# A cache page loaded into 32 partitions in pieces of 8 KB instead of 128 partitions in pieces of 2 KB

## The chip, the cores and the metric

The kernel runs on one core of one Trainium2 chip (trn2). The metric is the device time of one execution in microseconds (us). Three runs were timed before the change; the profile is of one further execution. TensorE is called PE, its weight load PEld, VectorE DVE, ScalarE ACT, GpSimd POOL and SyncE SP.

## What is computed

The reference is one inference step of a hybrid decoder layer: modulation of the input by a conditioning vector, one input projection, a short gated convolution beside differential attention with four heads, one output projection, two normalisations and a dense channel mixer. It does this for a prompt of 1,024 tokens and for eight sequences of four new tokens each. The eight sequences attend to 8,192 past keys each, which lie in pages of 128 keys; a table says which pages belong to a sequence. The part that matters here, cut:

```python
k_past = cache_k[l, page_table].reshape(bs, past, N_HEADS, 2, QK_HEAD)
v_past = cache_v[l, page_table].reshape(bs, past, N_HEADS, V_HEAD)
...
s = jnp.einsum('bqhcd,bkhcd->bhcqk', q, k).astype(jnp.float32) * (QK_HEAD ** -0.5)
p = jax.nn.softmax(s, axis=-1)
a = p[:, :, 0] - lam * p[:, :, 1]
return jnp.einsum('bhqk,bkhd->bqhd', a, v.astype(jnp.float32))
```

A page of keys is 128 rows of 512 float32 numbers (four heads of 128), 256 KB in one piece of memory; a page of values is the same. Eight sequences have 64 pages of either kind, so 1,024 pages or 268.4 MB are read.

## The kernel before

The kernel works in stages one after another: the modulation vectors; the input projection; the attention; the output projection; the channel mixer's first half; its second half. Only the attention stage reads the cache. There the prompt's attention and that of the eight sequences are woven into each other, written out by hand.

The attention stage is a row of eight steps. Step b scores the 64 key pages of sequence b and, beside that, weighs the 64 value pages of sequence b - 1 whose softmax is finished; step 0 has keys only, and after the last softmax there is a stretch with values only. Within a step the pages are taken in 16 groups of four, four rounds r of four groups g, and into each round one tile of the prompt's attention is woven. At the start of a step stands the softmax of the sequence before, a chain through DVE, PE and ACT.

Two rings hold the pages, `k_ring` (L230) and `v_ring` (L231), each of 128 partitions and four slots; a slot holds one group of four pages, 1 MB. The loads are issued by `load_pages` (L440). SP issues the groups with g = 0 and 2, POOL those with g = 1 and 3, each in the order keys of group g, values of group g, next g. Before every page the issuing engine reads its number from `page_row` (L445, a load from memory into a register); before the first page of a group it waits until the slot is free (L448); then it issues one load per page (L449). The four loads of a group raise the slot's semaphore by 16 each.

- `turn_keys` (L1428, its instruction L1432) waits until the four key pages of a slot are there, and turns them on DVE in blocks of 32 x 32 into `k_turned`; that frees the key slot.
- `key_group` (L845, its matmuls L852) multiplies the turned keys by the queries on PE, 32 matmuls for a group; ACT then copies the scores to `s_rows` (L1103).
- `value_group` (L857, its matmuls L862) waits until the four value pages of a slot are there and weighs them on PE by the turned scores `p_t`; that frees the value slot.

In the ring before, page j of a group lies in columns j of the slot, and key i of the page in partition i. Keys, scores, weights and values use that same place throughout, so which key of the group has which place doesn't matter as long as keys and values agree.

Two other loads are named below. `ada_bias` (L490) in the first stage is a vector of 6,144 numbers copied into 32 partitions, 24 KB each. `xs_rows` (L506) loads the 32 sample rows of 1,024 numbers into 32 partitions, 4 KB each; SP issues it after the prompt's rows `x_rows` (L504) and before the first weights `w_raw` (L500), which both go to all partitions.

Of the kernel before, what the change touches and what calls it, by code (L numbers as in the profile page):

```python
# [34 lines left out]
ds = bass.ds  # L35

P = 128
QUAD = 32
BANK = 512
# [72 lines left out]
def build(nc, z, io, const_at, n_const):  # L112
    T, D, B, S, H, HD, F = z.T, z.D, z.B, z.S, z.H, z.HD, z.F
# [5 lines left out]
    GP, RING = 4, 4  # L119
    REVS = z.PAGES // (GP * RING)  # L120
    NEW0 = z.PAGES * QUAD
    SC = NEW0 + QUAD
    assert z.MODS * D // BANK == 2 * z.MODS
    NG = F // WB
    NB_IN, NB_OUT = z.IN // WB, D // WB
    lam_init = 0.8 - 0.6 * math.exp(-0.3 * 0)
# [1 line left out]
    with ExitStack() as ctx:  # L128
# [311 lines left out]
        def load_pages(eng, par):  # L440


            def group(pages, ring, landed, free, b, r, g):
                for j in range(GP):
                    page = eng.value_load(page_row[0:1, ds((b * REVS + r) * (RING * GP) + (g * GP + j), 1)],  # L445
                                          min_val=0, max_val=z.POOL - 1)
                    if j == 0:
                        eng.wait_ge(free, (b * REVS + r) * RING + g + 1)  # L448
                    eng.dma_start(ring[:, g, j, :], pages[ds(page, 1)].rearrange("o p d -> p (o d)")  # L449
                                  ).then_inc(landed[g], 16)  # L450

            keys, values = (k_pages, k_ring, k_in, k_free), (v_pages, v_ring, v_in, v_free)
            with eng.Fori(0, REVS) as r:
                for g in range(par, RING, 2):
                    group(*keys, 0, r, g)
            with eng.Fori(0, B - 1) as b:
                with eng.Fori(0, REVS) as r:
                    for g in range(par, RING, 2):
                        group(*keys, b + 1, r, g)
                        group(*values, b, r, g)  # L460
            with eng.Fori(0, REVS) as r:
                for g in range(par, RING, 2):
                    group(*values, B - 1, r, g)
# [1237 lines left out]
```

## Time and profile before

| | us |
|---|---|
| median of 3 runs | 2386.14 (2381.53 to 2386.65) |
| span of the profiled execution, first to last instruction | 2380.2 |
| attention stage in it, from the first page ordered to the last value matmul | 428 to 1300 |
| PE busy | 1984.2 (83%) |
| DVE busy | 1056.3 (44%) |
| POOL busy | 354.0 (15%) |

The profile follows one execution. Times in its rows are from the start of the span. The columns of the views are told where each first stands. A row on transfers counts what all 16 DMA engines moved; their busy share is a mean over the 16 and counts a packet from its start to its end in the slice in which it starts, so that short slices can show more than 1. The time to landing of a load runs from its issue until its semaphore has its full count.

### The profile page before, as it was taken

To read this page: it belongs to the slowest core of one execution; us is meant where nothing else is said; L and a number is where in the kernel's file an instruction comes from. 1 tells how busy PE (TensorE), PEld (TensorE's weight loads), DVE (VectorE), ACT (ScalarE), POOL (GpSimd) and SP (SyncE) were. 2 spreads that over 40 slices of the span, in tenths; PEclk is the share of its full clock that TensorE was granted. 3 is DMA by queue.
4 is the path that set the end of the run, shared out by engine and by line. 5 is a ranking of instruction groups with operands and counts; after the bars stand their busy time and mean duration, and the time that the engine had idled before them with its cause. 6 is when DMAs were issued, how large, how long until landed. Compare 5 with 4: busy or idle time off the path is not lost.

```text
span 2380.2 us, 47877 instructions
## 1 busy us (share of the span) xinstructions
PE 1984.2 (83%) x17492; PEld 1635.0 (69%) x17492; DVE 1056.3 (44%) x1528; ACT 486.3 (20%) x831; POOL 354.0 (15%) x544
## 2 busy tenths in 40 slices
PE   4699999668786876878785794999999997999992
PEld 1277898557665765767674793777777776888881
DVE  2424211666675665766561557111111112455457
ACT  0300111021212112121221203111211111333331
POOL 0000000223242423324232104200000000000003
PEclk7799999799897988889796896999999998999996
DMA  9711223779897979879896410121212123411112
GB/s 302 256 36 35 72 71 118 250 245 341 285 385 282 385 279 346 314 283 381 298 354 234 156 35 18 54 71 53 88 53 70 53 88 128 137 41 37 36 32 91
DMA packets 210968, 404.21 MB, mean 170 GB/s; under 512 B 24426, under 2 KB 88938, under 8 KB 210788
## 3 DMA queue, kind: packets, MB, share of 16 engines
q1 hardware_dynamic: 161012, 261.51, 31.9%
q0 software_dynamic: 41488, 136.35, 15.5%
q10 hardware_dynamic: 8320, 4.19, 0.6%
q8 instruction: 116, 1.90, 0.3%
q14 instruction: 32, 0.26, 0.0%
HBM read 377.53 MB, written 24.51 MB: 169 GB/s over the span
## 4 chain that ended last, share of the span: by engine, by line
PE 65%; DVE 13%; SPq 7%; DMA 7%; issue 6%; ACT 1%; DVEq 0%; ACTq 0%
PE psum L753 26%; PE psum L1002 11%; PE psum L761 10%; PE psum L852 5%; DVE k_turned L1432 4%; SPq L445 4%; SPq L449 3%; DMA ada_w<-w_ada 3%; DMA k_ring<-cache_k 3%; PE psum L1009 2%; PE psum L862 2%; DVE p_t L424 2%; PE psum L736 2%; PE psum L832 1%; DVE x_lo L1282 1%
## 5 line engine op out<-in xcount | busy, mean ns | idle before, releaser
L852 PE MATMUL psum<-k_turned,q_blocks 128*32 128x128 f32 x4096 | 332.3, 286 | 85.6 <-DVE k_turned L1432 84.9
L852 PEld LDWEIGHTS psum<-k_turned,q_blocks 128*32 128x32 f32 x4096 | 291.7, 114 | 137.1 <-issue 98.5
L1432 DVE STREAM_TRANSPOSE k_turned<-k_ring 128x2048 f32<-128x2048 f32 x128 | 295.4, 2308 | 6.6 <-DMA k_ring<-cache_k 5.7
L753 PE MATMUL psum<-x_hi,w_hi 128*128 128x512 f32 x896 | 281.3, 395 | 0.0
L753 PE MATMUL psum<-x_lo,w_hi 128*128 128x512 f32 x896 | 277.3, 391 | 0.0
L753 PE MATMUL psum<-x_hi,w_lo 128*128 128x512 f32 x896 | 276.0, 389 | 0.0
L1301 DVE TENSOR_TENSOR w_lo<-w_raw,w_hi 128x2048 fp32r<-128x2048 f32 x37 | 86.9, 2350 | 363.1 <-ACT w_hi L1057 353.5
L1002 PE MATMUL psum<-d_hi,h_hi 128*128 128x256 f32 x704 | 209.2, 297 | 12.2 <-DVE d_lo L1646 11.1
L862 PE MATMUL psum<-v_ring,p_t 128*32 128x128 f32 x4096 | 191.7, 295 | 19.3 <-DMA v_ring<-cache_v 18.9
L1002 PE MATMUL psum<-d_lo,h_hi 128*128 128x256 f32 x704 | 199.9, 284 | 0.0
L1002 PE MATMUL psum<-d_hi,h_lo 128*128 128x256 f32 x704 | 199.7, 284 | 0.0
L753 PEld LDWEIGHTS psum<-x_hi,w_hi 128*128 128x128 f32 x896 | 165.6, 188 | 44.8 <-ACT h_out L1193 4.5
L449 POOL DMA_DIRECT2D k_ring<-cache_k x256 | 138.5, 541 | 371.5 <-issue 189.0
L753 PEld LDWEIGHTS psum<-x_lo,w_hi 128*128 128x128 f32 x896 | 168.8, 188 | 35.7
L753 PEld LDWEIGHTS psum<-x_hi,w_lo 128*128 128x128 f32 x896 | 168.5, 188 | 35.9
L761 PE MATMUL psum<-w_hi,x_hi 128*128 128x256 f32 x640 | 182.4, 285 | 0.0
L761 PE MATMUL psum<-w_hi,x_lo 128*128 128x256 f32 x640 | 181.3, 283 | 0.0
L761 PE MATMUL psum<-w_lo,x_hi 128*128 128x256 f32 x640 | 181.2, 283 | 0.0
L1645 DVE TENSOR_TENSOR h_lo<-h_all,h_hi 128x1024 fp32r<-128x1024 f32 x88 | 107.6, 1223 | 145.8 <-ACT d_hi L1218 145.8
L449 POOL DMA_DIRECT2D v_ring<-cache_v x256 | 138.4, 541 | 217.6 <-issue 170.0
L1002 PEld LDWEIGHTS psum<-d_hi,h_hi 128*128 128x128 f32 x704 | 135.1, 192 | 48.2 <-issue 45.0
L862 PEld LDWEIGHTS psum<-v_ring,p_t 128*32 128x32 f32 x4096 | 147.7, 117 | 27.9 <-DMA v_ring<-cache_v 25.8
(228 smaller groups left out, 2525.1 us busy)
## 6 DMA issues: line engine op xcount, KB each, us to landing
k_ring<-cache_k SPq DMA_DIRECT2D x256, 256.0 KB, 8.0
k_ring<-cache_k POOLq DMA_DIRECT2D x256, 256.0 KB, 6.1
v_ring<-cache_v SPq DMA_DIRECT2D x256, 256.0 KB, 8.8
v_ring<-cache_v POOLq DMA_DIRECT2D x256, 256.0 KB, 6.0
ada_w<-w_ada SPq DMA_DIRECT2D x12, 2048.0 KB, 9.6
w_raw<-w_in SPq DMA_DIRECT2D x12, 1024.0 KB, 5.3
w_raw<-w_gate SPq DMA_DIRECT2D x11, 1024.0 KB, 5.4
w_raw<-w_up SPq DMA_DIRECT2D x11, 1024.0 KB, 6.3
```

The costliest lines, as they stand in the source:

```text
L424: last = copy(to[QUAD * a:QUAD * (a + 1), :, j], got[:, :, :, a, :])
L445: page = eng.value_load(page_row[0:1, ds((b * REVS + r) * (RING * GP) + (g * GP + j), 1)], min_val=0, max_val=z.POOL - 1)
L449: eng.dma_start(ring[:, g, j, :], pages[ds(page, 1)].rearrange("o p d -> p (o d)")).then_inc(landed[g], 16)
L736: last = mm(psum[q:q + QUAD, 4 + s, 0:WB], x_t_s[:, k, :], w_raw[:, s, k, :], start=k < 4, stop=k >= KC - 4)
L753: last = mm(psum[:, 2 * ft + c, 0:CH], w[:, s, k, ft * P:(ft + 1) * P], x[:, k, c * CH:(c + 1) * CH], start=k == 0 and j == 0, stop=k == K ...
L761: last = mm(psum[:, t % TB, 0:WB], x[:, k, t * P:(t + 1) * P], w[:, s, k, :], start=k == 0 and j == 0, stop=k == KC - 1 and j == 2)
L852: last = mm(psum[QUAD * h:QUAD * (h + 1), g % 2, 0:GP * QUAD], q_blocks[:, h, d, :], k_turned[:, g % 2, :, h * HD + d * QUAD:h * HD + (d + ...
L862: last = mm(psum[QUAD * h:QUAD * (h + 1), 2, 0:P], p_t[:, (r * RING + g) * GP + j, :], v_ring[:, g, j, h * HD:(h + 1) * HD], start=False, ...
L1002: last = mm(psum[:, down_bank(par, pair), (t % 2) * WB:(t % 2 + 1) * WB], x[:, s, t * P:(t + 1) * P], w[:, s, :], start=k == 0 and j == 0 ...
L1301: v.tensor_tensor(w_lo[:, s], w_raw[:, s], w_hi[:, s], ALU.subtract).then_inc(w_lo_done, 1)
L1432: v.transpose(k_turned[:, g % 2].rearrange("p j n -> p (j n)"), k_ring[:, g].rearrange("p j n -> p (j n)")).then_inc(k_free, 1)
L1645: v.tensor_tensor(h_lo[:, s, :], h_all[:, k, :], h_hi[:, s, :], ALU.subtract)
```

## The change

A load of a page writes 32 partitions in place of 128. Page j of a group goes to partitions 32 j to 32 j + 31, and each of these partitions takes four consecutive key rows, 8 KB, which fill its whole slot. So a group of four pages still fills the same slot of 1 MB, and the four pages stand below one another rather than beside one another. A load has 32 pieces of 8 KB where it had 128 of 2 KB. No instruction of PE, DVE or ACT is added, removed, moved or changed in shape; SP and POOL issue as many loads as before in the same order with the same waits.

```diff
-    assert z.MODS * D // BANK == 2 * z.MODS
+    assert z.MODS * D // BANK == 2 * z.MODS and z.PAGE == QUAD * GP
...
-                    eng.dma_start(ring[:, g, j, :], pages[ds(page, 1)].rearrange("o p d -> p (o d)")
-                                  ).then_inc(landed[g], 16)
+                    eng.dma_start(ring[QUAD * j:QUAD * (j + 1), g].rearrange("p i d -> p (i d)"),
+                                  pages[ds(page, 1)].rearrange("o (p i) d -> (o p) (i d)", i=GP)).then_inc(landed[g], 16)
```

The constants are QUAD = 32 and GP = 4, the pages of a group.

## Rows read from the trace of the kernel before

**Rows 1.** The page: span, and data rate in 40 equal slices of it.

```profile
span 2380.2 us, 47877 instructions
...
GB/s 302 256 36 35 72 71 118 250 245 341 285 385 282 385 279 346 314 283 381 298 354 234 156 35 18 54 71 53 88 53 70 53 88 128 137 41 37 36 32 91
```

**Rows 2.** Stretches: us, busy time by engine, PE's clock, DMA share, GB/s.

```profile
428.00:523.00 95.00, 62.57 (x641) 50.57 (x642) 65.66 (x91) 15.01 (x43) 26.82 (x49) 0.90 0.84 280
523.00:619.00 96.00, 76.80 (x1157) 64.51 (x1155) 63.35 (x90) 18.16 (x48) 32.31 (x61) 0.92 0.91 327
...
931.00:1043.00 112.00, 83.38 (x1192) 70.12 (x1192) 66.69 (x102) 21.07 (x57) 35.63 (x66) 0.88 0.90 327
...
428.00:1300.00 872.00, 652.66 (x9338) 545.12 (x9342) 533.95 (x770) 165.29 (x439) 278.01 (x513) 0.88 0.88 316
```

**Rows 3.** Stretches within a step: streaming, then the softmax, then the start again.

```profile
570.00:630.00 60.00, 47.70 (x669) 40.42 (x665) 37.41 (x48) 14.77 (x37) 22.59 (x42) 0.97 1.03 383
630.00:640.00 10.00, 2.74 (x42) 1.96 (x42) 7.96 (x21) 1.12 (x2) 0.00 (x0) 0.55 0.02 9
640.00:645.00 5.00, 4.85 (x61) 4.22 (x62) 2.91 (x5) 0.32 (x2) 0.54 (x1) 0.54 0.58 153
```

**Rows 4.** DMA from 560 to 620 us: packets, then queues (q0 POOL, q1 SP).

```profile
DMA packets 9697, 23.13 MB, mean 386 GB/s; under 512 B 1403, under 2 KB 1403, under 8 KB 9688
...
q0 software_dynamic: 3680, 12.06, 53.0%
q1 hardware_dynamic: 6008, 10.94, 49.9%
```

**Rows 5.** Line L1432, the key transpose: what it waits for, who waits for it.

```profile
  DMA k_ring<-cache_k: 5.7, 7
...
  POOL k_ring L449: 182.5, 17
```

**Rows 6.** Waits of the whole span: waiting, waited for, us, times, longest.

```profile
PEld psum L862 <- DMA v_ring<-cache_v: 25.8, 20, 5.7
...
PE psum L862 <- DMA v_ring<-cache_v: 18.9, 11, 5.4
```

**Rows 7.** Loads in order of time on POOL; line L449, SP (ns min/median/max).

```profile
562.80 0.54 POOL L449 DMA_DIRECT2D k_ring<-cache_k  x1 [1.22 <-issue]
564.04 0.54 POOL L449 DMA_DIRECT2D k_ring<-cache_k  x1 [0.70 <-issue]
...
L449 SPq DMA_DIRECT2D k_ring<-cache_k x256: 332/333/916, 428.7 to 1217.2; - x128
```

**Rows 8.** The bias: its issue (KB, us to landing), then stretches as in rows 2.

```profile
ada_bias<-b_ada SPq DMA_DIRECT2D x1, 768.0 KB, 6.4
...
21.00:22.00 1.00, 0.00 (x0) 0.00 (x0) 0.19 (x1) 0.00 (x0) 0.00 (x0) 1.00 1.37 394
22.00:24.50 2.50, 0.00 (x0) 0.00 (x0) 1.54 (x9) 0.20 (x1) 0.00 (x0) 0.77 0.77 157
```

**Rows 9.** Stretches around the sample rows' transfer, columns as in rows 2.

```profile
93.00:93.50 0.50, 0.50 (x3) 0.38 (x2) 0.00 (x0) 0.02 (x2) 0.00 (x0) 1.00 1.01 401
...
94.00:94.50 0.50, 0.50 (x2) 0.14 (x2) 0.00 (x0) 0.23 (x2) 0.00 (x0) 1.00 0.97 205
94.50:95.00 0.50, 0.50 (x2) 0.02 (x1) 0.00 (x0) 0.43 (x1) 0.00 (x0) 1.00 1.10 299
95.00:95.50 0.50, 0.50 (x2) 0.20 (x2) 0.00 (x0) 0.18 (x1) 0.00 (x0) 1.00 1.09 246
95.50:96.00 0.50, 0.50 (x2) 0.00 (x0) 0.00 (x0) 0.40 (x1) 0.00 (x0) 1.00 1.08 305
96.00:97.00 1.00, 0.14 (x1) 0.01 (x1) 0.00 (x0) 0.57 (x1) 0.00 (x0) 1.00 1.09 344
```

**Rows 10.** DMA from 428 to 1300 us: packets, and one kind of issue.

```profile
DMA packets 121564, 275.21 MB, mean 316 GB/s; under 512 B 16502, under 2 KB 22646, under 8 KB 121464
...
k_ring<-cache_k SPq DMA_DIRECT2D x256, 256.0 KB, 8.0
```

**Rows 11.** PE in order of time: a key group amid streaming, one after a softmax.

```profile
561.78 2.13 PE L852 MATMUL psum<-k_turned,q_blocks 128*32 128x128 f32 x29
...
640.15 3.85 PE L852 MATMUL psum<-k_turned,q_blocks 128*32 128x128 f32 x29 [2.09 <-DVE k_turned L1432]
```

## The prediction

> **What bounds the kernel now.** The reading goes from the whole to the place of the change. The page gives a span of 2380.2 us, and its slices of data rate stand near 380 only in the second quarter, the stage that reads the paged cache [rows 1]. The table by stretch cuts that stage, 428 to 1300 us, into its eight steps and a stretch with values alone: 872 us, of which the seven steps in the middle take 96 to 112 us each [rows 2]. Such a step moves 64 key pages and 64 value pages of 262,144 bytes, 33.55 MB, and in the part of it that streams, the 16 DMA engines are busy without a gap: 383 GB/s at a busy share of 1.03 over 60 us, then some 10 us at 9 GB/s while the softmax of a sequence holds back the ring's slots [rows 3]. At 386 GB/s [rows 4], 33.55 MB take 87 us. So transfers alone fill 87 of about 103 us.
>
> They are not the only limit. The wait rows of the key transpose show it idle for key pages during only 5.7 us in the whole stage, while the loads wait 182.5 us on POOL for slots that the transpose has yet to free [rows 5]. PE waits for value pages mainly at the very end of the stage, 25.8 and 18.9 us on its two rows [rows 6]. So before the change arithmetic and transfers run almost level: a transfer that becomes cheaper can win little, one that becomes dearer is felt as soon as a step's transfer exceeds about 100 us, that is below 33.55 MB / 100 us = 335 GB/s.
>
> **The change part by part.** What it removes: nothing is issued less often. The same 1,024 loads of 256 KB go out on SP and POOL in the same order, with the same slots, waits and semaphores. Keys change their places inside a group of four pages, but key and value pages alike, so no later instruction changes its shape. The order of keys in the softmax sums has no cost.
>
> *Issue.* A page goes out on POOL every 1.22 us (562.80 to 564.04 and on), of which 0.54 us describe the 128 pieces; on SP the instruction lasts 0.33 us [rows 7]. Were the description of 32 pieces free, POOL would save at most 0.54 us a page. It buys nothing by itself: two queues at 1.22 us offer 2 x 262,144 / 1.22 = 430 GB/s, above the 386 that the engines take. I count zero; the cover is the engines' own full row of work, and if it were gone the 0.54 us would be the bound of the gain.
>
> *Larger pieces.* In the 60 us of streaming, SP's queue took 49.9% of 16 engines for 10.94 MB in 2 KB pieces and POOL's 53.0% for 12.06 MB in packets twice that size [rows 4]: 43.8 against 42.2 us of engine time per MB. Bringing SP's 134 MB to POOL's price saves 134 x 1.6 / 16 = 13 us of transfer over the stage, and one further halving of the same fixed part on all 268.4 MB saves about 268.4 x 0.8 / 16 = 13 us. That is at most 27 us of transfer time, 4%, and only where transfers are waited for.
>
> *Fewer partitions per load.* This is the dear part. All loads of the cache in the trace of before go to 128 partitions, so I look for loads into 32. There are two large enough. The first is the bias of the first stage, 32 rows of 24 KB. From 22.0 to 24.5 us it is alone on the engines, half of it, and the row has 157 GB/s at a busy share of 0.77: 204 GB/s while the engines work [rows 8]. Busy, they move half of what they move elsewhere. The opening microsecond of it has 394 at 1.37, that is 288, which I read as a start with nothing queued ahead. The second is the 32 sample rows of 4 KB, queued between two loads that use all partitions. The rate is 401 before it, then 205, 299, 246 and 305 while it mixes with its successor, then 344, and the engines stay fully busy throughout [rows 9]. The bias rows are 32 copies of one source, the sample rows are 32 different ones; what they share is the destination of 32 partitions. So the loss goes with the destination and not with the source.
>
> After the change every page is such a load. Pages 0 to 3 of a group go to four different quarters, and SP and POOL each have one page in work. Where both pages hinder each other as the bias hinders itself, the rate is 204. Where they lie apart, the nearest row is the mixed stretch, mean of the four rows 264. I give each half of the bytes: 1 / (0.5/204 + 0.5/264) = 230 GB/s. No row shows two such loads side by side, so 204 and the 386 of now stay as ends.
>
> The Trainium skill, page "SBUF — State Buffer", section "Door 1: The DMA port swizzle", gives the reason: partitions 0 to 31 reach only 8 of the 16 ports by which transfers enter, 32 to 63 the same 8, the upper 64 the others, and 32 partitions are held to about 218 GB/s. The bias row agrees at 204. The same page says of two transfers on the two halves that together they gained only 6%; no row here shows that. By it, 218 and 231 in place of 204 and 264 give 224 GB/s and an estimate of 2740 us.
>
> *The sum.* The stage moves 275.21 MB, of which 1,024 pages are 268.4 MB [rows 10]. At 230 GB/s the pages take 1167 us. The remaining 6.8 MB at the old rate take 18 us. The pauses of today close: between the last value page of a step and the first slot freed lie some 20 us, and the rings then have about 7 MB ordered, 30 us of work at 230. What stays uncovered is the start (4 us) and the softmax of the last sequence, after which only the value ring of 4 MB is ordered, some 8 us: 12 us. Sum 1197 us against 872, so +325 us; 2380 + 325 = 2705 in the profiled execution. The median of the runs stands 6 us above that span, so **2710 us**.
>
> With 204: 1316 + 18 + 12 = 1346, +474, 2860. With 264: 1017 + 18 + 35 (pauses reopen to about 3 us a step) = 1070, +198, 2584.
>
> *PE's clock.* When PE waits more, its clock may fall. The 29 matmuls of a key group took 2.13 us at 561.78 us, and 3.85 us at 640.15 us, after a softmax, with the clock at 0.54 in that stretch, its lower level of 1.2 GHz for most of it [rows 3, 11]. Sixteen groups at the lower level add 28 us to a step of about 100 us of arithmetic, still within the 146 us that 33.55 MB take at 230. I count zero, and a push upwards where the rate is at 264 and the cover is 127 us.
>
> **The rivals.** *A: the halves overlap.* The two queues settle on different partitions and what one leaves free the other uses. For it: in a group half of the pages go to the other half of the partitions, and the mixed row reaches 299 and 305 in two of its four entries. Against it: it also falls to 205 and 246. At 300 GB/s the pages take 895 us, with 18 us and some 60 us of pauses 973, +101: 2487. The case spans 2400 to 2580.
>
> *B: faster.* The loss seen with the bias and the sample rows belongs to a single load, and with eight or more pages ordered on two queues the engines find work for all partitions; then 8 KB pieces win. It decides from 335 GB/s upwards, and its price is bounded by what is waited for: 5.7 us on the key transpose, and of the value waits at the stage's end 4% of the last 30 us or so, 1 us, plus earlier slots after each softmax, perhaps 1 us in each of eight. About -10 us, 2376; all of the 27 us would give 2359. Against it stands that the busy engines fall to 204 in the bias row although 16 of them work.
>
> The Trainium skill, page "DMA: Bandwidth & Descriptors", section "Why small descriptors are slow", speaks for B: about 3 cycles are lost per packet, which is 4% of a 2 KB piece and 1% of an 8 KB one. By it an estimate of 16 us of transfer is saved, near the 27 above.
>
> *C: no change.* The rate stays between 335 and 400 and arithmetic sets the step: 2386.
>
> *D: worse than the bias row.* Under load the two queues disturb each other and the rate drops below 200, as to 180: 1491 + 30 = 1521, +649, 3035.
>
> **How the numbers follow.** Forecast, 204 to 264 GB/s: 0.70, at 2710. A: 0.16. B: 0.05. C: 0.04. D: 0.05. The range keeps the forecast whole with its high end of 2860 and a little for a slower PE, 2880, and takes in the greater part of A down to 2500; B, C, the rest of A and D stay out, about 0.18. Within 0.2%, about what a measurement of this kernel can tell from no change, is C: 0.04; faster is B: 0.05; slower is the rest: 0.91.
>
> **What would show it.** In the profile after: the rate over a step between 200 and 265 GB/s with the engines' busy share still near 1.0; time to landing of the pages up from 6 to 9 us to about 25 to 30 us (4 MB ordered per queue at half of 230); the key transpose idle for key pages during some 200 us or more in place of 5.7; POOL's wait for slots no longer in 17 large pieces after each softmax; no pause in transfers at the softmax but the last; every other stage as long as before. Wrong would be: the streaming rows at 300 or more (A), at 380 or more with steps of about 100 us (B or C), or packets of the old sizes in the queue rows.

## The result and the profile after

The changed kernel takes 2720.44 us, median of four runs (2688.72 to 2729.59), against 2386.39 us (2381.53 to 2387.13, four runs) before: a ratio of 1.1365, 95% interval 1.1296 to 1.1433. It is slower by 14%, and the forecast was 2710. Ratios leave out a run that lies more than 1.5% above the fastest of its kernel, here that of 2729.59, so that they can differ from the quotient of the medians. One execution was profiled; it took 2712.41 us.

The page of the changed kernel: span, data rate in 40 equal slices, and the shares of the chain of work that ended last, by engine and by line. Then the chain of the kernel before, by engine.

```profile
span 2710.8 us, 47877 instructions
...
GB/s 310 180 47 47 63 108 191 216 245 263 225 225 216 211 222 241 233 214 213 239 252 249 256 190 156 34 13 62 78 62 73 61 52 77 167 83 39 32 40 80
...
PE 54%; DMA 27%; DVE 9%; issue 5%; SPq 2%; ACT 1%; POOL 1%; POOLq 1%; DVEq 0%; ACTq 0%
PE psum L753 23%; DMA v_ring<-cache_v 23%; PE psum L1002 10%; PE psum L761 9%; PE psum L852 3%; DMA ada_w<-w_ada 2%; PE psum L862 2%; PE psum L1009 2%; DVE k_turned L1432 2%; DVE p_t L424 1%; PE psum L736 1%; DVE x_lo L1282 1%; SPq L445 1%;
```

```profile
PE 65%; DVE 13%; SPq 7%; DMA 7%; issue 6%; ACT 1%; DVEq 0%; ACTq 0%
```

The slices of the attention stage never reach the 341 to 385 that six of them had in [rows 1]; most lie between 211 and 263. And the chain now runs through the value pages' transfers for 23% of the span, where all transfers together had 7% of it before.

Stretches of the changed kernel, columns as in [rows 2]: the stages before the attention, the attention, the stages after it.

```profile
0.00:428.00 428.00, 366.96 (x2336) 289.55 (x2336) 115.89 (x165) 60.23 (x89) 0.22 (x5) 0.92 0.37 125
428.00:1630.00 1202.00, 763.82 (x9382) 602.05 (x9382) 537.71 (x771) 165.53 (x439) 255.06 (x513) 0.79 1.00 229
1629.00:2710.80 1081.80, 966.51 (x5790) 799.70 (x5779) 406.07 (x593) 260.78 (x303) 76.12 (x26) 0.94 0.21 69
```

The attention stage lasts 1202 us in place of 872 [rows 2], 330 us more, and the span grew by 2710.8 - 2380.2 = 331 us: all but a microsecond or two of the loss is there. From 1629 us, the last value matmuls, to the end of the program it takes 1081.8 us, where it took 2380.2 - 1300 = 1080.2. In the stage the DMA engines are busy at a share of 1.00 (0.88 before) and move 229 GB/s (316 before).

What the engines carry, from 600 to 660 us, as in [rows 4] (q0 is POOL's queue, q1 SP's), and the time to landing of one kind of load over the whole program, with the issue on POOL (ns min/median/max):

```profile
DMA packets 2882, 15.81 MB, mean 263 GB/s; under 512 B 957, under 2 KB 957, under 8 KB 957
...
q0 software_dynamic: 1436, 7.83, 51.2%
q1 hardware_dynamic: 1440, 7.89, 50.5%
```

```profile
L449 POOL DMA_DIRECT2D k_ring<-cache_k x256: 492/492/520, 432.5 to 1516.2; - x128
...
DMA to landing us min/median/max: 3.3/22.6/34.2
```

The pieces are larger, as the diff says: the two queues have 2,876 packets for 15.7 MB, where [rows 4] have 9,688 for 23.0. Yet a megabyte now takes 50.5% of 16 engines x 60 us / 7.89 = 61 us of engine time on SP's queue, and took 43.8. The engines are occupied all the time and get less done. A key page lands 22.6 us after its issue, in the median over both queues; from SP it took 8.0 [rows 10], from POOL 6.1.

What the key transpose waits for and who waits for it, then the two rows of PE's waits for value pages (us, times, longest), as in [rows 5, 6]:

```profile
  DMA k_ring<-cache_k: 177.0, 61
...
  POOL k_ring L449: 411.4, 49
```

```profile
PEld psum L862 <- DMA v_ring<-cache_v: 204.9, 82, 6.0
...
PE psum L862 <- DMA v_ring<-cache_v: 177.8, 78, 5.7
```

Key pages held the transpose up for 5.7 us before and do so for 177.0 now; value pages held PE up for 25.8 and 18.9 us on its two rows and do so for 204.9 and 177.8. The readers wait for pages through the whole stage, the key transpose 61 times in place of 7.

### The profile page after: what moved, and what is told of

The parts are those of the page before. It is cut to its first block, busy times and chain, and to the rows that moved or that the text cites. A ratio compares the mean times of both kernels' runs of the same rounds, so it can differ in the third digit from the quotient of the medians.

```text
span 2710.8 us, 47877 instructions
## 1 busy us (share of the span) xinstructions
PE 2096.6 (77%) x17492; PEld 1691.1 (62%) x17492; DVE 1059.5 (39%) x1528; ACT 486.5 (18%) x831; POOL 331.4 (12%) x544
## 4 chain that ended last, share of the span: by engine, by line
PE 54%; DMA 27%; DVE 9%; issue 5%; SPq 2%; ACT 1%; POOL 1%; POOLq 1%; DVEq 0%; ACTq 0%
PE psum L753 23%; DMA v_ring<-cache_v 23%; PE psum L1002 10%; PE psum L761 9%; PE psum L852 3%; DMA ada_w<-w_ada 2%; PE psum L862 2%; PE psum L1009 2%; DVE k_turned L1432 2%; DVE p_t L424 1%; PE psum L736 1%; DVE x_lo L1282 1%; SPq L445 1%; PE psum L881 1%; DMA k_ring<-cache_k 1%
## 5 line engine op out<-in xcount | busy, mean ns | idle before, releaser
L852 PE MATMUL psum<-k_turned,q_blocks 128*32 128x128 f32 x4096 | 383.5, 314 | 134.8 <-DVE k_turned L1432 134.1
L852 PEld LDWEIGHTS psum<-k_turned,q_blocks 128*32 128x32 f32 x4096 | 323.9, 126 | 208.7 <-issue 144.2
L1432 DVE STREAM_TRANSPOSE k_turned<-k_ring 128x2048 f32<-128x2048 f32 x128 | 295.5, 2309 | 177.1 <-DMA k_ring<-cache_k 177.0
L862 PE MATMUL psum<-v_ring,p_t 128*32 128x128 f32 x4096 | 189.2, 321 | 178.9 <-DMA v_ring<-cache_v 177.8
L862 PEld LDWEIGHTS psum<-v_ring,p_t 128*32 128x32 f32 x4096 | 141.1, 127 | 209.6 <-DMA v_ring<-cache_v 204.9
L449 POOL DMA_DIRECT2D k_ring<-cache_k x256 | 126.0, 492 | 567.5 <-DVE k_turned L1432 401.6
L1103 ACT COPY s_rows<-psum 128x128 f32<-128x128 f32 x128 | 34.1, 266 | 773.3 <-PE psum L852 773.3
L449 POOL DMA_DIRECT2D v_ring<-cache_v x256 | 128.0, 500 | 365.1 <-PE psum L862 210.2
```

Of the source, the lines that this page charges most:

```text
L449: eng.dma_start(ring[QUAD * j:QUAD * (j + 1), g].rearrange("p i d -> p (i d)"), pages[ds(page, 1)].rearrange("o (p i) d -> (o p) (i d)", i ...
L852: last = mm(psum[QUAD * h:QUAD * (h + 1), g % 2, 0:GP * QUAD], q_blocks[:, h, d, :], k_turned[:, g % 2, :, h * HD + d * QUAD:h * HD + (d + ...
L862: last = mm(psum[QUAD * h:QUAD * (h + 1), 2, 0:P], p_t[:, (r * RING + g) * GP + j, :], v_ring[:, g, j, h * HD:(h + 1) * HD], start=False, ...
L1103: copy(s_rows[:, (r * RING + g) * (GP * QUAD):(r * RING + g + 1) * (GP * QUAD)], psum[:, g % 2, 0:GP * QUAD]).then_inc(s_bank_free, 1)
L1432: v.transpose(k_turned[:, g % 2].rearrange("p j n -> p (j n)"), k_ring[:, g].rearrange("p j n -> p (j n)")).then_inc(k_free, 1)
```

## The experiments

Theory H says that a load's rate goes with the partitions that it reaches: 32 or 64 neighbouring ones give some 200 GB/s, and two loads side by side gain only if they lie in different halves of the partitions, 0 to 63 and 64 to 127. Its first rival, P, says that the shape of the pieces does it: 32 pieces of 8 KB, whatever partitions they go to. Diffs are against the changed kernel, and ratios against the kernel before, measured on the same chip as the kernel in question.

**e1_probe: rates by themselves.** Ahead of the first page stand trials, each of eight pages (2.1 MB) on one queue or on each of both (four pages for the 16 partitions), and each waits for the one before. All else is the changed kernel.

```diff
+            def rows32(first, n0):
+                return [(flat(ring[first:first + QUAD, g]), page(n0 + n, 4)) for n, (ring, g) in enumerate(slots)]
...
+            spread = [(flat(ring[0:P:4, g]), page(n, 4)) for n, (ring, g) in enumerate(slots)]
...
             sp.wait_ge(pages_in, 16)
+            probes(sp, 0)
             load_pages(sp, 0)
```

> The changed kernel with a row of trial loads ahead of its first page, each row waited for before the next, nothing else running on the transfers: eight pages at a time, by SP alone, by POOL alone or by both, in the form of before, of after, and of shapes between. The time itself (some 150 us longer than 2720) says nothing; the rates of the rows do. Theory H (the loss goes with the partitions that a load reaches, one half of them being one bottleneck): 128 partitions in 2 KB pieces about 370 to 390 GB/s; 32 partitions about 204, whether 0 to 31 or 64 to 95 and whether in 8 KB or 2 KB pieces; 64 neighbouring partitions no more than 210; 64 or 32 partitions spread over all 128 well above 204; 16 partitions about 100; 8 KB pieces on 128 partitions 390 or more; SP and POOL on 0 to 31 and 32 to 63 at once about 204, on 0 to 31 and 64 to 95 at once 264 to 390. Rival P (the loss goes with the pieces, two of 8 KB for each engine): 32 partitions in 2 KB pieces back at 380, 64 neighbouring partitions in 4 KB about 280, 8 KB pieces on 128 partitions about 204 like after, spread 32 partitions 204.

Stretches inside the trials, columns as in [rows 2]; the last two numbers are the engines' busy share and GB/s. On SP alone: partitions 64 to 95 in 8 KB pieces; 0 to 31 in 2 KB pieces; 0 to 63 in 4 KB pieces; every second partition in 4 KB pieces; every fourth partition in 8 KB pieces; all 128 in 8 KB pieces (whole groups of four pages); 0 to 15. On both queues: 0 to 31 beside 32 to 63; 0 to 31 beside 64 to 95. On POOL alone: 0 to 31; all 128 in 2 KB pieces.

```profile
454.00:463.00 9.00, 0.00 (x0) 0.00 (x0) 0.00 (x0) 0.00 (x0) 0.00 (x0) 0.50 1.03 208
466.00:475.00 9.00, 0.00 (x0) 0.00 (x0) 0.00 (x0) 0.00 (x0) 0.00 (x0) 0.50 1.06 210
479.00:488.00 9.00, 0.00 (x0) 0.00 (x0) 0.00 (x0) 0.00 (x0) 0.00 (x0) 0.50 1.03 201
491.00:496.00 5.00, 0.00 (x0) 0.00 (x0) 0.00 (x0) 0.00 (x0) 0.00 (x0) 0.50 0.90 308
500.00:505.00 5.00, 0.00 (x0) 0.00 (x0) 0.00 (x0) 0.00 (x0) 0.00 (x0) 0.50 0.84 290
509.00:513.50 4.50, 0.00 (x0) 0.00 (x0) 0.00 (x0) 0.00 (x0) 0.00 (x0) 0.50 0.95 399
516.00:524.00 8.00, 0.00 (x0) 0.00 (x0) 0.00 (x0) 0.00 (x0) 0.00 (x0) 0.50 0.93 98
542.00:560.00 18.00, 0.00 (x0) 0.00 (x0) 0.00 (x0) 0.00 (x0) 1.76 (x4) 0.50 1.03 204
565.00:580.00 15.00, 0.00 (x0) 0.00 (x0) 0.00 (x0) 0.00 (x0) 1.37 (x3) 0.50 1.03 243
585.00:593.00 8.00, 0.00 (x0) 0.00 (x0) 0.00 (x0) 0.00 (x0) 1.10 (x3) 0.50 1.04 206
598.00:603.00 5.00, 0.00 (x0) 0.00 (x0) 0.00 (x0) 0.00 (x0) 1.48 (x3) 0.50 0.87 315
```

Loads into 32 neighbours run at 208, at 210 with small pieces, and at 206 from POOL; 64 neighbours are no better, 201; 16 give 98. The same 8 KB pieces to every fourth partition give 290 in a short trial with its ends, 290 / 0.84 = 345 while the engines work. So the price lies in the destination being neighbours, not in the number of pieces, their size or the queue, and P falls. Three trials have no row here: all partitions on SP, which ran beside another load; 0 to 31 in 8 KB pieces on SP, 181 at a busy share of 0.92; and all partitions in 2 KB pieces on both queues, 374. Two loads in the same half share 204; in different halves they reach 243, a fifth more and not double, and less than the 264 to 390 that theory H had expected. The Trainium skill, page "SBUF — State Buffer", section "Door 1: The DMA port swizzle", gives a port by bits 2 to 4 and bit 6 of a partition's number; every fourth partition then meets all 16 ports, 0 to 63 only 8, and the 345 against 201 agrees.

**e2_small_pieces: the same 32 partitions, four pieces of 2 KB to each.**

```diff
-                    eng.dma_start(ring[QUAD * j:QUAD * (j + 1), g].rearrange("p i d -> p (i d)"),
-                                  pages[ds(page, 1)].rearrange("o (p i) d -> (o p) (i d)", i=GP)).then_inc(landed[g], 16)
+                    eng.dma_start(ring[QUAD * j:QUAD * (j + 1), g],
+                                  pages[ds(page, 1)].rearrange("o (i p) d -> (o p) i d", i=GP)).then_inc(landed[g], 16)
```

> One part of the change alone: each page still goes to 32 neighbouring partitions, but in 128 pieces of 2 KB as before (key i of a page to partition i mod 32). Theory H: as slow as after or a little slower, 2700 to 2800 us, rate 205 to 260 GB/s. Rival P (piece size): back to before, 2386 us within 20, rate 380 in the streaming stretches.

It took 2759.2 us (2755.17 to 2771.81), ratio 1.1589 (1.1552 to 1.1626). With 128 pieces of the old size the loss is still there, and larger by 39 us. Beside other work, too, it goes with the partitions; the 8 KB pieces help.

**e3_spread: 8 KB pieces, page j of a group to partitions j, j + 4, j + 8 and on.**

```diff
-                    eng.dma_start(ring[QUAD * j:QUAD * (j + 1), g].rearrange("p i d -> p (i d)"),
+                    eng.dma_start(ring[j:P:GP, g].rearrange("p i d -> p (i d)"),
```

> The other part alone: 32 partitions in 8 KB pieces, but every fourth partition (page j to partitions j, j+4, ...), so that one load reaches all of the partitions' range. Theory H: the loss is gone for the greater part, 2370 to 2450 us, rate 330 to 400 GB/s. Rival P: as after, 2690 to 2730 us.

It took 2372.4 us (2369.35 to 2381.67, ten runs), ratio 0.9955 (0.9943 to 0.9967): faster than both kernels, by 0.45% than the one before. Of this kernel the stage and a streaming stretch, then its DMA from 560 to 620 us, then the key transpose's waits:

```profile
428.00:1290.00 862.00, 649.37 (x9358) 545.14 (x9362) 533.58 (x770) 165.54 (x439) 266.43 (x513) 0.89 0.85 319
565.00:620.00 55.00, 47.05 (x727) 39.62 (x718) 35.97 (x46) 9.61 (x25) 22.35 (x44) 1.00 1.00 394
```

```profile
DMA packets 4335, 23.78 MB, mean 396 GB/s; under 512 B 1439, under 2 KB 1439, under 8 KB 1439
...
q0 software_dynamic: 2255, 12.36, 52.9%
q1 hardware_dynamic: 2072, 11.31, 47.1%
```

```profile
  DMA k_ring<-cache_k: 1.6, 1
...
  POOL k_ring L449: 181.1, 19
```

Loads with 32 pieces into 32 partitions run at 396 GB/s on two queues, above the 386 of [rows 4], and the key transpose waits 1.6 us for pages. The whole loss of the change is undone by the stride of the destination alone; that shows the cause. By the queue rows a megabyte costs 0.529 x 16 x 60 / 12.36 = 41.1 us of engine time on POOL's queue and 40.0 on SP's (42.2 and 43.8 before), so 134 MB on each save an estimate of 134 x (1.1 + 3.8) / 16 = 41 us of transfer; the stage's rows, busy share times length, give 0.88 x 872 - 0.85 x 862 = 35. The kernel gains 13. That the rest is hidden behind arithmetic, as the prediction's first part said of any cheaper transfer, fits the chain of this stage, which has PE and DVE in front (under e7_spread_small); no run shows it by itself.

**e7_spread_small: every fourth partition, four pieces of 2 KB to each.**

```diff
-                    eng.dma_start(ring[QUAD * j:QUAD * (j + 1), g].rearrange("p i d -> p (i d)"),
-                                  pages[ds(page, 1)].rearrange("o (p i) d -> (o p) (i d)", i=GP)).then_inc(landed[g], 16)
+                    eng.dma_start(ring[j:P:GP, g],
+                                  pages[ds(page, 1)].rearrange("o (i p) d -> (o p) i d", i=GP)).then_inc(landed[g], 16)
```

> The spread form (every fourth partition), but in 2 KB pieces: tells where the 0.45% of the spread form against before come from. If from the 8 KB pieces: 2383 to 2400 us, like before or slower. If from the spread or from the issue alone: 2372 us within 4.

It took 2406.81 us (2403.99 to 2410.3), ratio 1.0103 (1.0085 to 1.012). A streaming stretch of it:

```profile
565.00:620.00 55.00, 45.96 (x720) 38.41 (x721) 37.91 (x47) 8.88 (x24) 22.59 (x42) 1.00 1.03 378
```

The same stretch has 394 in e3_spread. Next, SP's load of a key page (ns min/median/max) and the chain from 428 to 1290 us by line, in e3_spread and then in this run:

```profile
L449 SPq DMA_DIRECT2D k_ring<-cache_k x256: 472/472/710, 429.2 to 1215.1; - x128
...
by line: PE psum L852 22.8%; DVE k_turned L1432 15.0%; issue 11.9%; PE psum L862 7.4%; DVE p_t L424 4.7%; PE psum L832 4.2%; PE psum L818 3.9%; SPq L449 3.9%; SPq L445 3.5%; PE psum L881 2.9%; DVE soft L1383 2.2%; DMA v_ring<-cache_v 2.1%; 
```

```profile
L449 SPq DMA_DIRECT2D k_ring<-cache_k x256: 602/603/1262, 431.8 to 1249.6; - x128
...
by line: SPq L449 20.8%; SPq L445 15.3%; issue 14.5%; PE psum L852 8.2%; DVE k_turned L1432 7.8%; DVE p_t L424 4.7%; DMA v_ring<-cache_v 4.0%; PE psum L832 2.8%; PE psum L881 2.7%; DMA k_ring<-cache_k 2.6%; PE psum L862 2.5%; PE psum L818 1
```

So e3's gain comes with the 8 KB pieces: 2407 to 2372, 34 us between these two, and the spread by itself is no gain over 128 partitions. But the 34 us are not the price of a transfer alone. SP's instruction lasts 0.60 us here and 0.47 in e3_spread, 0.33 before [rows 7], and SP's two lines, the page number and the load, carry 36% of the chain here and 7% there: in this run the issue sets much of the pace. It is 1% slower than loads that are just as small but reach 128 partitions, and slower than the 2383 to 2400 that were expected; the longer instruction on SP is the likely cause, and no run tries it alone.

**e4_half: pages of 64 neighbouring partitions, 4 KB pieces, halves in turn.**

```diff
+                    half, side = P // 2, j % 2
+                    eng.dma_start(ring[half * side:half * (side + 1), g, j // 2 * 2:j // 2 * 2 + 2].rearrange("p i d -> p (i d)"),
+                                  pages[ds(page, 1)].rearrange("o (p i) d -> (o p) (i d)", i=2)).then_inc(landed[g], 16)
```

> Between the two forms: a page to 64 neighbouring partitions in 4 KB pieces, pages 0 and 2 to the lower half, 1 and 3 to the upper. Theory H: 64 neighbouring partitions are no better than 32, so 2600 to 2730 us (halves alternate with every page, which may help the two queues to differ). Rival P or a loss that shrinks evenly with the number of partitions: half way, 2480 to 2560 us.

It took 2607.03 us (2581.7 to 2617.94), ratio 1.0901 (1.0833 to 1.0968). A long stretch of its stage, and the same of the changed kernel:

```profile
460.00:1200.00 740.00, 506.29 (x6410) 405.85 (x6405) 381.38 (x538) 115.60 (x308) 185.73 (x358) 0.84 1.01 252
...
460.00:1200.00 740.00, 481.23 (x5849) 381.92 (x5850) 351.90 (x505) 107.78 (x289) 160.56 (x325) 0.82 1.01 228
```

The loss shrinks by a third, but 64 neighbours stay far from the 383 of [rows 3], as H expects, and 2480 to 2560, half-way, is not reached. This edit changes two things, the number of partitions and the order of the halves, which now alternate with every page. That the number is not what counts rests on e1_probe, 201 for 64 neighbours; the order alone moves the rate too (e9_probe_order).

**e5_by_half and e6_same_half: which partitions the two queues have in work.** Both split every group between the queues: by half, SP has pages 0 and 1 (the lower half) and POOL 2 and 3; same half, SP has 0 and 2 and POOL 1 and 3, so that both begin in the lower half and both go on to the upper. The readers wait for both queues' semaphores. The diff is that of by half; same half has `(par, par + 2)` in its place.

```diff
-                for j in range(GP):
+                for j in (2 * par, 2 * par + 1):
...
-                for g in range(par, RING, 2):
+                for g in range(RING):
```

> Form of after, but the two queues divide each group by partitions: SP loads pages 0 and 1 of every group (lower half of the partitions), POOL pages 2 and 3 (upper half), so the two never write to the same half. Theory H with the trial rows (203 GB/s on one half, 233 on two): the rate never falls to 205, and the pages take 268.4 MB / 0.233 = 1152 us or less, 2560 to 2690 us in all. Rival Q (the rate differs between the steps of after, 211 to 264, for another reason, such as where the pages lie in memory): as after, 2700 to 2730 us, and again steps between 210 and 265.

> The counterpart: SP loads pages 0 and 2 of every group, POOL pages 1 and 3, so that the two queues, if they keep pace, are always in the same half. Theory H: near the rate of one half, 203 to 215 GB/s throughout, 268.4 MB / 0.205 = 1309 us, 2780 to 2860 us. Rival Q: as after, 2700 to 2730 us.

By half took 2631.75 us (2616.94 to 2653.03), ratio 1.1067 (1.0997 to 1.1136); same half 2666.25 us (2651.01 to 2709.15), ratio 1.1161 (1.1121 to 1.1202). The stage's middle in e5_by_half, in e6_same_half and in the changed kernel:

```profile
460.00:1460.00 1000.00, 666.75 (x8607) 549.06 (x8609) 511.73 (x722) 155.48 (x414) 231.49 (x472) 0.85 1.01 250
```

```profile
460.00:1460.00 1000.00, 663.04 (x8397) 544.52 (x8398) 498.87 (x708) 152.04 (x408) 227.04 (x463) 0.83 1.02 243
```

```profile
460.00:1460.00 1000.00, 653.14 (x7928) 515.82 (x7928) 473.70 (x679) 146.49 (x390) 216.30 (x437) 0.81 1.02 230
```

Different halves on the two queues give 250 where the changed kernel has 230, and the intervals of these two ratios lie apart. But e6_same_half gains as well, with 243, and its interval touches that of e5_by_half. So dividing every group between the queues helps; that the halves do it is not shown by these two runs. e6_same_half was forecast at 2780 to 2860, near the 204 of two loads in one half, and came out faster than the changed kernel. That expectation failed. It supposed that the queues stay in step; nothing holds them there, and one page of lag puts them into opposite halves. That they did lag was not shown.

**e8_after_again: the changed kernel, unchanged, a second profile.** In the first profile the rate differs from step to step. Rival Q: it belongs to the pages that a step reads, and the same step shows the same rate again.

> The changed kernel once more, for a second profile: whether the rates of its seven steps (262, 225, 213, 241, 213, 252 and 257 GB/s in the first profile, 20 us stretches in the middle of each) belong to the steps or to the execution. Theory H with a rate that depends on how the 16 engines and the two queues happen to stand to each other: other rates at the same steps, within 203 to 290. Rival Q (where the pages lie in memory): the same rates at the same steps, within 5 GB/s.

It took 2698.08 us. The same stretches in the first profile (first fence) and in this one:

```profile
640.00:680.00 40.00, 25.66 (x289) 20.62 (x289) 18.68 (x27) 10.94 (x27) 8.08 (x16) 0.83 1.03 264
...
900.00:940.00 40.00, 24.68 (x279) 18.15 (x277) 14.57 (x16) 3.65 (x9) 8.21 (x16) 0.79 1.03 212
...
1200.00:1240.00 40.00, 25.00 (x283) 18.78 (x282) 14.76 (x18) 3.65 (x9) 8.46 (x17) 0.79 1.02 213
```

```profile
640.00:680.00 40.00, 26.01 (x313) 21.64 (x309) 20.07 (x29) 11.91 (x28) 8.23 (x16) 0.87 1.02 289
...
900.00:940.00 40.00, 27.86 (x327) 20.97 (x329) 18.34 (x21) 4.81 (x12) 9.31 (x19) 0.83 1.03 254
...
1200.00:1240.00 40.00, 23.70 (x271) 17.25 (x268) 14.24 (x18) 3.75 (x9) 8.51 (x17) 0.83 1.03 215
```

One step repeats within 2 GB/s, another moves from 212 to 254, with the same pages. So the pages that a step reads don't set the rate by themselves; Q, which asked for the same rates within 5, falls, if a page lies at the same place in memory in both executions, which no row shows. Of seven steps four repeat within about 10, so a part of it may belong to them.

**e9_probe_order: the order of the loads.** Trials as in e1_probe, of 32 pages with 8 KB pieces into 32 neighbouring partitions.

> The changed kernel with eight longer trial rows ahead of its first page, 32 loads of 32 partitions each (8.4 MB), nothing else on the transfers; only the rates of the rows count. First SP alone: pages in the order of after (two to the lower half, two to the upper, and again), in turn (lower, upper, lower, upper), all lower and then all upper, and the first order once more. Then both queues, 16 loads each: as after, divided by half, divided so that both are in the same half, and as after with POOL beginning in the upper half. Theory D (the 16 engines drift apart within a queue, so that those ahead find the other half free): all lower and then all upper stays at 203 but for its middle; the order of after begins near 205 and rises, to 230 or more; in turn higher still; same half rises as well, which would explain the 2666 us of that kernel. Rival (the halves mix only between the two queues): SP alone 203 in every order, same half 203, by half 233 or more.

Stretches inside the trials. SP alone: lower and upper half in turn; all of the lower half, then all of the upper; the changed kernel's order. Both queues: as the changed kernel has them; by half; same half; as the changed kernel, but POOL begins each group in the upper half.

```profile
479.00:512.00 33.00, 0.00 (x0) 0.00 (x0) 0.00 (x0) 0.00 (x0) 0.00 (x0) 0.50 1.03 229
518.00:554.00 36.00, 0.00 (x0) 0.00 (x0) 0.00 (x0) 0.00 (x0) 0.00 (x0) 0.50 1.03 204
561.00:596.00 35.00, 0.00 (x0) 0.00 (x0) 0.00 (x0) 0.00 (x0) 0.00 (x0) 0.50 1.02 217
603.00:630.00 27.00, 0.00 (x0) 0.00 (x0) 0.00 (x0) 0.00 (x0) 3.63 (x8) 0.50 1.02 249
640.00:668.00 28.00, 0.00 (x0) 0.00 (x0) 0.00 (x0) 0.00 (x0) 3.20 (x7) 0.50 1.03 247
676.00:708.00 32.00, 0.00 (x0) 0.00 (x0) 0.00 (x0) 0.00 (x0) 3.61 (x8) 0.50 1.03 222
716.00:750.00 34.00, 0.00 (x0) 0.00 (x0) 0.00 (x0) 0.00 (x0) 3.87 (x9) 0.50 1.02 207
```

On one queue the order moves the rate between 204 and 229, so the rival, SP alone at 203 in every order, falls; the changed kernel's order stood there twice, at 217 and, from 458 to 470 us, at 218. Theory D, engines that drift apart within a queue, fits the ranking of the orders, but the rise that it expected within the changed kernel's order, from 205 to 230, did not come: its slices of 4 us lie between 205 and 227 from start to end. On two queues the same loads ran at 249 and at 207 with only POOL's starting page changed. Each of these ran once, and the changed kernel itself moves from 212 to 254 in one order, so that the starting page does it is not shown. Trials without readers, with no slot to wait for, thus span 207 to 249, and most of the changed kernel's slices lie in or near that span. Which of the two a step gets would hang on how the queues happen to stand, which fits rates that differ between executions; it is an argument, since no trace row shows the standing of the queues, and 289 in the step above exceeds every trial with neighbours.

## Why the prediction was right, step by step

- **The reading of the bound.** Right. Arithmetic and transfers ran level, and only a rate below about 335 GB/s would be felt: 394 in e3_spread won 13 us, 229 cost 330.
- **Issue at zero.** Right. POOL's instruction went from 0.54 to 0.49 us, and POOL waits for slots, 411.4 us in 49 times, not for its own work.
- **Larger pieces.** The mechanism was right, the term probably too small: up to 27 us of transfer was forecast; e3_spread's queue rows give 41, its stage's rows 35. In the kernel's time it is worth 39 us among neighbours, where transfers set the pace (e2_small_pieces to the change; the latter's runs spread over 41 us themselves). The 34 us from e7_spread_small to e3_spread hold SP's longer issue too. In the changed kernel it is part of the 229.
- **Few partitions, the lower end.** Right: 204 from the bias row, 204 to 210 in the trials. That the loss goes with the destination was read from two rows that had little else in common; e3_spread shows it, and that neighbours are what matters.
- **The upper end and the mean.** Right in the result, and that was in part luck. 264 came from a stretch where a load into 32 partitions mixed with one into all 128. Two loads in different halves reach 243, and the share of the bytes that is so placed was chosen, not read. The mean of 230 was met, 229 over the stage; by the trials it is the middle of a span from 207 to 249. The 6% that the Trainium skill gives for two transfers on two halves over a single one (page "SBUF — State Buffer", section "Can I just issue two DMAs to hit both halves?") were 17% in e1_probe, 243 on two queues against 208 on one; by its figures the estimate was 2740, the measurement 2720.
- **The sum.** 1197 us for the stage, measured 1202; 2705 for the span, measured 2710.8.
- **Pauses.** Right. The softmaxes within the stage no longer stop the transfers; the lowest 10 us among them, from 1140 us, still have 183 GB/s. The last one does; the row of the changed kernel:

```profile
1560.00:1570.00 10.00, 4.00 (x58) 3.83 (x60) 6.10 (x12) 4.66 (x9) 0.00 (x0) 0.67 0.02 7
```

- **PE's clock.** Counted at zero, and it shows no price. The granted clock of the stage fell from 0.88 to 0.79 as PE waited more, and PE's busy time rose from 653 to 764 us, but the engines' busy share of 1.00 leaves little room in which transfers could have waited for PE.
- **Signs.** Landing was forecast at 25 to 30 us and is 22.6 in the median, 34.2 at most. The transpose's wait was put at some 200 or more and is 177. Both fall somewhat short. The other stages are as long as before.
- **Rivals.** A (300 GB/s, 2487) did not come about, though its mechanism is real in part: the halves overlap by a fifth. B and C needed 335 and fell; e3_spread shows what B would have been. D needed less than 200; the 16 slices of the page that lie wholly within the streaming part have 211 or more.

What stays open: what sets the rate between 207 and 289 when two queues load neighbours, and from it the changed kernel's own spread of 1.5% between runs, where the kernel before has 0.2%.

## What to carry to other kernels

Before a load is given fewer, longer pieces, look at which partitions it still reaches: neighbours cost nearly half of the rate, a stride over the whole range does not, and only there did the longer pieces pay on the whole. A small load elsewhere in the same program, at half the rate while the engines worked, was enough to find the lower end of the price ahead. And a transfer that was level with arithmetic gives back little when it gets cheaper and most of it when it gets dearer: by busy share times length, 13 of 35 us here against 330 of 1.00 x 1202 - 0.88 x 872 = 435.

## What the runs showed of the hardware

- A load into 32 partitions reaches 345 GB/s while busy if they are every fourth one, and 208 if they are neighbours (e1_probe); with both queues at work, 396 in a streaming stretch (e3_spread) beside 229 over the changed kernel's stage and 250 over the middle of e5_by_half's.
- Two queues with the same loads in two orders ran at 249 and at 207, once each (e9_probe_order). Both rows have a busy share of 1.02, which says nothing of the rate at which the engines work.
- POOL's instruction for a page hardly shrinks with the pieces: 0.54 us for 128, 0.49 for 32. SP's goes with the stride as well: 0.33 us for 128 pieces into 128 partitions, 0.32 for 32 into 32 neighbours, 0.47 for 32 into every fourth partition and 0.60 for 128 there (before, the changed kernel, e3_spread, e7_spread_small).
